# One decoder layer on one core: where the input and PLE tiles are turned, who makes the low parts of the second norm, and the loop order of the last gate

## The reference, cut to what matters

```python
x = x + (g_a * (y_a @ w_br_moba) + g_b * (y_b @ w_br_nsa)) @ w_o     # two branches, merge gates, output projection
u = causal_dwconv(rms_norm(x, ffn_norm) @ w_up, conv_w, conv_b)      # second norm, up projection, conv of 3
u_act, u_lin = split(u, 2)
x = x + (gelu(u_act) * u_lin) @ w_down
x = x + sigmoid(x @ w_ple_gate) * (p @ w_ple)                        # p is (512, 256)
```

## Time and profile before

| | us |
|---|---|
| median of 3 runs (lowest, highest) | 994.91 (992.62, 996.42) |
| the profiled execution | 993.43 |
| its span | 991.6 |
| TensorE busy in the span | 913.8 (92%) |
| VectorE, ScalarE, GpSimd busy | 485.4, 405.8, 381.8 |

### The profile page before, as it was taken

One profiled execution on the slowest core, in us unless ns is written; L12 is line 12 of the kernel. 1 busy time (PEld: TensorE's weight loads), 2 busy tenths in 40 slices (PEclk: granted clock), 3 DMA queues, 4 the chain that ended last, 5 costly groups with the idle time before them and its releaser, 6 DMA issues.

```text
span 991.6 us, 13260 instructions
## 1 busy us (share of the span) xinstructions
PE 913.8 (92%) x4581; PEld 779.1 (79%) x4581; DVE 485.4 (49%) x1145; ACT 405.8 (41%) x849; POOL 381.8 (38%) x360
## 2 busy tenths in 40 slices
PE   7898798786989889998989899999999999999988
PEld 7896688686978777877767678888888888888866
DVE  6616766767686677786431433444333342011132
ACT  5121554444454445554334354544444453232320
POOL 4723312303031211124545475444544445464540
PEclk9999899999989989999999999999999999999999
DMA  5745222214111212334554334333333333332232
GB/s 165 178 110 138 64 62 70 72 36 114 44 33 54 75 54 75 100 128 164 182 169 130 117 112 135 94 95 96 88 108 103 98 94 103 99 96 85 85 97 84
DMA packets 98917, 99.33 MB, mean 100 GB/s; under 512 B 15940, under 2 KB 73252, under 8 KB 98852
## 3 DMA queue, kind: packets, MB, share of 16 engines
q1 hardware_dynamic: 98799, 98.48, 33.9%
q10 hardware_dynamic: 53, 0.01, 0.0%
HBM read 87.58 MB, written 10.88 MB: 99 GB/s over the span
## 4 chain that ended last, share of the span: by engine, by line
PE 78%; DVE 12%; issue 4%; ACT 4%; DMA 1%; POOL 0%; SPq 0%; POOLq 0%; ACTq 0%; DVEq 0%
PE banks L1411 24%; PE banks L1413 23%; PE banks L1412 23%; DVE plain_arena L1161 2%; PE banks L1542 2%; PE banks L1460 1%; DVE plain_arena L1189 1%; DVE split_arena L1080 1%; DVE split_arena L1234 1%; PE banks L1525 1%; PE banks L1524 1%; ACT split_arena L836 1%; PE banks L1484 1%; DMA plain_arena<-in_x_dram 1%; ACT plain_arena L824 1%
## 5 line engine op out<-in xcount | busy, mean ns | idle before, releaser
L1411 PE MATMUL banks<-split_arena 128*128 128x512 f32 (+4 forms) x1224 | 471.3, 385 | 15.7 <-POOL split_arena L652 4.1
L1413 PE MATMUL banks<-split_arena 128*128 128x512 f32 (+4 forms) x1224 | 459.1, 375 | 0.0
L1412 PE MATMUL banks<-split_arena 128*128 128x512 f32 (+4 forms) x1224 | 458.6, 375 | 0.0
L652 POOL TENSOR_TENSOR split_arena<-plain_arena,split_arena 128x512 fp32r<-128x512 f32 x184 | 238.7, 1309 | 248.5 <-ACT split_arena L852 248.5
L1411 PEld LDWEIGHTS banks<-split_arena 128*128 128x128 f32 x1224 | 234.6, 192 | 58.8 <-issue 12.4
L1413 PEld LDWEIGHTS banks<-split_arena 128*128 128x128 f32 x1224 | 233.4, 191 | 36.3
L1412 PEld LDWEIGHTS banks<-split_arena 128*128 128x128 f32 x1224 | 234.5, 192 | 32.7
L852 ACT ACTIVATE split_arena<-plain_arena 128x512 fp32r<-128x512 f32 x184 | 113.3, 628 | 196.3 <-PE banks L1413 187.8
L824 ACT ACTIVATE plain_arena<-plain_arena 128x128 f32<-128x128 f32 (+1 forms) x96 | 53.9, 561 | 135.7 <-DVE plain_arena L1189 135.5
L1372 DVE SCALAR_TENSOR_TENSOR plain_arena<-banks,plain_arena 128x511 f32<-128x511 f32 x44 | 32.7, 744 | 135.3 <-ACT plain_arena L954 135.3
L620 POOL TENSOR_TENSOR split_arena<-plain_arena,split_arena 128x512 fp32r<-128x512 f32 x16 | 26.5, 1655 | 155.8 <-ACT split_arena L910 143.5
(11 more groups left out here) (158 smaller groups left out, 868.1 us busy)
## 6 DMA issues: line engine op xcount, KB each, us to landing
plain_arena<-in_w_up_dram SPq DMA_DIRECT2D x88, 256.0 KB, 3.2
plain_arena<-in_w_down_dram SPq DMA_DIRECT2D x44, 256.0 KB, 2.6
plain_arena<-in_w_in_dram SPq DMA_DIRECT2D x18, 512.0 KB, 4.4
plain_arena<-in_w_in_dram SPq DMA_DIRECT2D x32, 192.0 KB, 3.3
plain_arena<-in_x_dram SPq DMA_DIRECT2D x8, 512.0 KB, 4.7
gates<-plain_arena SPq DMA_DIRECT2D x16, 256.0 KB, 2.0
plain_arena<-skew SPq DMA_DIRECT2D x16, 256.0 KB, 3.7
plain_arena<-gates SPq DMA_DIRECT2D x16, 256.0 KB, 3.7
```

Source lines behind the costliest of these rows:

```text
L652: pool.tensor_tensor(W2l[:, c % RING, :], raw2[:, c % RING, :], W2h[:, c % RING, :].bitcast(F32), ALU.subtract).then_inc(w2_lo, 1)
L1411: nc.tensor.matmul(o, ah, bh, start=first, stop=False)
L1412: nc.tensor.matmul(o, ah, bl, start=False, stop=False)
L1413: return nc.tensor.matmul(o, al, bh, start=False, stop=last)
```

## The change

**x and p.** Tiles 0 and 1 of x are loaded into the columns of `x1T` that belong to tokens 256 to 511, as soon as attention no longer needs that memory (`turned` T). They are turned ahead of chunks 10 and 11, the first into banks 4 and 5, the second into banks 6 and 7, both behind `brB_done` 4. Tile 2 uses `xs` and is turned ahead of step 2 of `wo` half 0 behind `brB_done` 8, p is turned ahead of step 3 into banks 6 and 7, tile 3 (buffer `xg`) ahead of step 5. The first chunk of branch B, half 1, now waits for four copies to `x1T` instead of two, and p is loaded at chunk 19 behind the second turned tile. **The second norm.** GpSimd waits, ahead of its split of chunk 39, until four low parts of the norm are made (`h2_lo` 4). These low parts, and those ahead of the last gate, are now made by VectorE. The sum of squares has one wide add less on VectorE, and `token_sums` takes the last tile of squares with four further matmuls. **The last gate.** ScalarE splits the chunk ahead of the tanh. Half 1 goes depth step by depth step over the four token tiles, the last of them as two halves of 256 columns (banks 7 and 0), and its last two steps tile by tile. The end has nine pieces instead of eight.

The diff, without unchanged lines, and without the renamed semaphores, banks and indices in `take_x`, `pTl` and the stores (which go over the same nine pieces):

```diff
@@ -154,6 +154,7 @@
     RING = 8
+    TAIL = [(k, slice(0, S)) for k in range(7)] + [(7, slice(0, 256)), (7, slice(256, 512))]
@@ -391,6 +392,21 @@
     return ("k", n % 2, x - 2) if n < 4 else ("k", (n - 4) // 2, x - 2)
...
+def x_again(tt):
...
+    if tt < 2:
+        return x1T[:, :, (2 + tt) * P:(3 + tt) * P]
+    return (xs if tt == 2 else xg).rearrange("p (k c) -> p k c", k=KT)
...
+p_nat = x1T[:, :, 3 * P:4 * P]
...
+def tail_bank(k, cs):
...
+    return k if cs.start == 0 else 0
...
+def x_bank(tt):
+    return (4, 6, 4, 4)[tt]
@@ -535,22 +551,19 @@
-        if tt in (1, 3):
-            sp.wait_ge(xs_tr, tt if tt == 1 else 2)
-        if tt == 2:
-            sp.wait_ge(br_sum, 8)
-            sp.dma_start(xg, x_d[tt]).then_inc(xg_in, 16)
-        else:
-            sp.dma_start(xs, x_d[tt]).then_inc(xs_in, 16)
+        sp.dma_start(x_again(tt), x_d[tt].rearrange("p (k c) -> p k c", k=KT)).then_inc(xr_in[tt], 16)
...
+    sp.wait_ge(turned, T)
+    load_x(0)
+    load_x(1)
...
-    load_x(0)
+    load_x(2)
@@ -564,17 +577,15 @@
         if c == 19:
-            load_x(1)
+            sp.wait_ge(xs_tr, 2)
+            for tt in range(NT):
+                sp.dma_start(p_nat[:, 2 * tt:2 * tt + 2, :], p_d[tt].rearrange("p (k c) -> p k c", k=2)).then_inc(p_in, 16)
...
-            load_x(2)
+            sp.wait_ge(br_sum, 8)
...
-        if c == 28:
-            sp.wait_ge(xs_tr, 3)
-            for tt in range(NT):
-                sp.dma_start(xg[:, tt * PLE:(tt + 1) * PLE], p_d[tt]).then_inc(xg_in, 16)
@@ -711,6 +723,8 @@
                                    ALU.subtract).then_inc(yt_lo[0], 1)
+            if c == cidx[("wo", 1, KT - 1)] + RING:
+                pool.wait_ge(h2_lo, 4)
@@ -723,16 +737,6 @@
                         pool.tensor_tensor(sumsq, sumsq, sqt[:, kt % 2, :], ALU.add).then_inc(ssq_done, 1)
-        if c == cidx[("ple", 1, 0)] + 7:
-            for kt in range(KT):
-                pool.wait_ge(h2_hi, kt + 1)
-                pool.tensor_tensor(h2l[:, kt, :], hst[:, kt % 2, :], h2h[:, kt, :].bitcast(F32), ALU.subtract).then_inc(h2_lo, 1)
-        for mg in range(2):
-            if c == cidx[("dn", mg, NF - 1)] + 7:
-                for m in range(4):
-                    kt = 4 * mg + m
-                    pool.wait_ge(x2_hi, kt + 1)
-                    pool.tensor_tensor(h2l[:, kt, :], x1T[:, kt, :], h2h[:, kt, :].bitcast(F32), ALU.subtract).then_inc(x2_lo, 1)
@@ -973,21 +977,21 @@
     for c in range(RING, NC + 10):
-        if c == 11 + RING:
-            take_x(0)
...
+        if e in (10, 11):
+            take_x(e - 10)
...
-        if kind == "wo" and a == 0 and kt in (2, 4, 5):
-            take_x({2: 1, 4: 2, 5: 3}[kt])
-        if kind == "wo" and a == 0 and kt == 7:
+        if kind == "wo" and a == 0 and kt in (2, 5):
+            take_x({2: 2, 5: 3}[kt])
+        if kind == "wo" and a == 0 and kt == 3:
...
-                nc.scalar.activation(pTh[:, k, :], PS[:, 4 + k, :], ACT.Copy).then_inc(pT_hi, 1)
+                nc.scalar.activation(pTh[:, k, :], PS[:, 6 + k, :], ACT.Copy).then_inc(pT_hi, 1)
@@ -1023,21 +1027,20 @@
                 nc.scalar.activation(h2h[:, i, :], x1T[:, i, :], ACT.Copy).then_inc(x2_hi, 1)
+        if c < NC:
+            split_chunk(c)
...
-            for tt in range(NT):
-                k = 4 * a + tt
+            for k, cs in TAIL[:4] if a == 0 else TAIL[4:]:
...
-                    act.wait_ge(tail_done, tt + 1)
+                    act.wait_ge(tail_done, TAIL.index((k, cs)) - 3)
...
-                nc.scalar.activation(thb[:, k % 4, :], PS[:, 4 * a + tt, :], ACT.Tanh, scale=0.5).then_inc(th_done, 1)
-        if c < NC:
-            split_chunk(c)
+                nc.scalar.activation(thb[:, k % 4, cs], PS[:, tail_bank(k, cs), cs], ACT.Tanh, scale=0.5).then_inc(th_done, 1)
@@ -1343,12 +1346,12 @@
-    for a, b, n in ((0, 1, 6), (2, 3, 8)):
-        dve.wait_ge(x1_sq, n)
-        link(nc.vector.tensor_tensor(sqt[:, a, :], sqt[:, a, :], sqt[:, b, :], ALU.add))
-    link(nc.vector.tensor_tensor(sqt[:, 0, :], sqt[:, 0, :], sqt[:, 2, :], ALU.add))
+    dve.wait_ge(x1_sq, 6)
+    link(nc.vector.tensor_tensor(sqt[:, 0, :], sqt[:, 0, :], sqt[:, 1, :], ALU.add))
...
-    nc.vector.tensor_tensor(sumsq, sumsq, sqt[:, 0, :], ALU.add).then_inc(sq_summed, 1)
+    link(nc.vector.tensor_tensor(sumsq, sumsq, sqt[:, 0, :], ALU.add))
+    dve.wait_ge(x1_sq, 7)
+    nc.vector.tensor_tensor(sumsq, sumsq, sqt[:, 2, :], ALU.add).then_inc(sq_summed, 1)
@@ -1356,11 +1359,16 @@
     dve.wait_ge(bc_done, 1)
-    for i in range(KT):
-        if i >= 2:
-            dve.wait_ge(h2_lo, i - 1)
-        nc.vector.scalar_tensor_tensor(out=hst[:, i % 2, :], in0=x1T[:, i, :], scalar=cst[:, 8 + i:9 + i], in1=rbc,
-                                       op0=ALU.mult, op1=ALU.mult).then_inc(h2_f, 1)
+    for i in range(KT + 1):
+        if i < KT:
+            if i >= 2:
+                dve.wait_ge(h2_lo, i - 1)
+            nc.vector.scalar_tensor_tensor(out=hst[:, i % 2, :], in0=x1T[:, i, :], scalar=cst[:, 8 + i:9 + i], in1=rbc,
+                                           op0=ALU.mult, op1=ALU.mult).then_inc(h2_f, 1)
+        if i > 0:
+            kt = i - 1
+            dve.wait_ge(h2_hi, kt + 1)
+            nc.vector.tensor_tensor(h2l[:, kt, :], hst[:, kt % 2, :], h2h[:, kt, :].bitcast(F32), ALU.subtract).then_inc(h2_lo, 1)
@@ -1388,20 +1396,23 @@
             nc.vector.tensor_tensor(x1T[:, i, :], PS[:, 4 * mg + m, :], x1T[:, i, :], ALU.add).then_inc(x2_done, 1)
+        for kt in range(4 * mg, 4 * mg + 4):
+            dve.wait_ge(x2_hi, kt + 1)
+            nc.vector.tensor_tensor(h2l[:, kt, :], x1T[:, kt, :], h2h[:, kt, :].bitcast(F32), ALU.subtract).then_inc(x2_lo, 1)
...
-    for k in range(8):
+    for i, (k, cs) in enumerate(TAIL):
...
-        dve.wait_ge(th_done, k + 1)
+        dve.wait_ge(th_done, i + 1)
...
-        nc.vector.scalar_tensor_tensor(out=thb[:, k % 4, :], in0=thb[:, k % 4, :], scalar=1.0, in1=ppb[:, k % 4, :],
+        nc.vector.scalar_tensor_tensor(out=thb[:, k % 4, cs], in0=thb[:, k % 4, cs], scalar=1.0, in1=ppb[:, k % 4, cs],
...
-        dve.wait_ge(th_mul, k + 1)
+        dve.wait_ge(th_mul, i + 1)
...
-        o = x2n[:, tt, ng * 512:(ng + 1) * 512]
-        nc.vector.tensor_tensor(o, o, thb[:, k % 4, :], ALU.add).then_inc(o_done, 1)
+        o = x2n[:, tt, ng * 512 + cs.start:ng * 512 + cs.stop]
+        nc.vector.tensor_tensor(o, o, thb[:, k % 4, cs], ALU.add).then_inc(o_done, 1)
@@ -1631,36 +1642,30 @@
     def turn_x(tt):
-        if tt == 2:
-            pe.wait_ge(xg_in, 16)
-        else:
-            pe.wait_ge(xs_in, 16 * (tt + 1 if tt < 2 else 3))
-        src = xg if tt == 2 else xs
-        b = 4 + 2 * (tt % 2)
-        if tt == 0:
-            pe.wait_ge(brB_done, 4)
-        if tt >= 1:
-            pe.wait_ge(brB_done, 8)
-        if tt >= 2:
-            pe.wait_ge(xT_done, 2 * tt - 2)
+        pe.wait_ge(xr_in[tt], 16)
+        b = x_bank(tt)
+        pe.wait_ge(brB_done, 4 if tt < 2 else 8)
+        if tt == 3:
+            pe.wait_ge(xT_done, 6)
...
-            ins = nc.tensor.transpose(PS[:, b + kt // 4, P * (kt % 4):P * (kt % 4 + 1)], src[:, P * kt:P * (kt + 1)], ident)
+            ins = nc.tensor.transpose(PS[:, b + kt // 4, P * (kt % 4):P * (kt % 4 + 1)], x_again(tt)[:, kt, :], ident)
...
-        pe.wait_ge(xg_in, 16 * 5)
-        pe.wait_ge(xT_done, 8)
+        pe.wait_ge(p_in, 16 * NT)
+        pe.wait_ge(brB_done, 8)
...
-                ins = nc.tensor.transpose(PS[:, 4 + k, P * tt:P * (tt + 1)], xg[:, tt * PLE + P * k:tt * PLE + P * (k + 1)], ident)
+                ins = nc.tensor.transpose(PS[:, 6 + k, P * tt:P * (tt + 1)], p_nat[:, 2 * tt + k, :], ident)
...
-        pe.wait_ge(x1_done, KT)
+        pe.wait_ge(x1_sq, KT)
...
-            ins = nc.tensor.matmul(PS[:, 4, tt:tt + 1], sumsq[:, P * tt:P * (tt + 1)], ones[:, 0:1], start=True, stop=True)
+            nc.tensor.matmul(PS[:, 4, tt:tt + 1], sumsq[:, P * tt:P * (tt + 1)], ones[:, 0:1], start=True, stop=False)
+            ins = nc.tensor.matmul(PS[:, 4, tt:tt + 1], sqt[:, 3, P * tt:P * (tt + 1)], ones[:, 0:1], start=False, stop=True)
@@ -1685,16 +1690,14 @@
                 turn_probs(T + c - LAG)
-        if c == 10:
-            turn_x(0)
-        if (kind, a, kt) == ("wo", 0, 1):
-            turn_x(1)
+        if c in (10, 11):
+            turn_x(c - 10)
+        if (kind, a, kt) == ("wo", 0, 2):
+            turn_x(2)
...
-            turn_x(2)
+            turn_p()
...
-        if (kind, a, kt) == ("wo", 1, 0):
-            turn_p()
@@ -1723,7 +1726,7 @@
                 if a:
-                    pe.wait_ge(xT_done, 2)
+                    pe.wait_ge(xT_done, 4)
@@ -1734,6 +1737,7 @@
                     pe.wait_ge(pT_lo, 2)
+                    pe.wait_ge(xT_done, 8)
@@ -1783,13 +1787,21 @@
+    def last_gate(kt, k, cs):
...
+        w_, t_ = cidx[("pg", 1, kt)] % RING, slice(P * (k - 4), P * (k - 3))
+        if kt == 0 and tail_bank(k, cs) == 0:
```

(33 more changed lines are left out.)

2 lines of the change are left out of this document (1 added, 1 removed).

## The result

| | us |
|---|---|
| changed kernel, median of 4 runs (lowest, highest) | 979.61 (977.41, 981.22) |
| kernel before, same session, median of 4 | 993.76 (992.43, 996.42) |
| ratio | 0.9849, 95% interval 0.983 to 0.9867 |
| profiled execution, its span | 978.59, 976.8 |

The change is worth 14.8 us by the two profiled executions (14.2 by the medians). 980.4 was forecast.

What follows compares the result with a forecast made beforehand. TensorE's work (78% of the span) plus its halts was taken as the bound. Terms 3.4 + 2.0 + 2.8 + 5.5 = 13.7 us gave 979.7 from the profiled execution and 981.2 from the median; forecast 980.4, range 976 to 987.

Steps and rivals of the forecast that it cites:

- parts 1 and 2: Turning x tiles and p around branch B and `wo`: x gains 4.4 us and gives back 1.0, p gains 2.0.
- part 3: Second norm: GpSimd held, one add fewer, low parts on VectorE; `up` starts 2.8 us sooner, bounds 1.5 and 3.2.
- part 4: Last gate: early split and new loop order remove the 4.09 us halt; 5.5 us gained, between 4.9 and 5.9.
- Part 1, the second halt: TensorE's halt before `turn_x(1)` shrinks from 3.98 to 1.26 us, clock stays up: 2.7 plus 1.7, together 4.4 us.
- Part 1, the price in the DMAs: One more MB of x delays GpSimd's splits before the gate loads, blocking a VectorE add: 1.0 us lost, bounds 0 and 2.0.
- part 2: p turned five chunks earlier, removing the wait before `wo` half 1: 2.0 us gained, bounds 1.8 and 2.2.
- Both covers: In the first `up` chunks, splits of chunks 39 and 42 are ready 3 us before TensorE needs them.
- rival C: The hold stops TensorE in the first `up` chunks, 3 us of halt with a low clock behind: 985.5; chance 0.06.
- A: Clock falls at one of two halts remaining around the x turns, 1.7 us plus up to 1.5 more halt: 983.6; chance 0.14.
- B: In the last gate, matmuls of 256 columns cost as much as 512: 985.5; chance 0.05.
- D: Slower than before: x tiles crowd the queues, TensorE halts ahead of chunk 8; 1000 needs 4 + 19 us late; chance 0.02.
- E: At the second x turn `brB_done` 8 moves later by as much as TensorE gains, 4.4 us less: 984.8; chance 0.07.

Runs made afterwards that it cites:

- u3: Changed kernel with tile 2 of x turned ahead of step 1 of `wo` half 0 instead of step 2; ratio to the kernel before 0.9888.
- u2: Changed kernel without the hold of GpSimd ahead of its split of chunk 39; ratio to the kernel before 0.9839.
- u6: Changed kernel with the second norm's low parts on GpSimd at their old place and no hold; ratio to the kernel before 0.9859.
- i5: Changed kernel with x tile 1 loaded behind the load of chunk 15 and tile 2 behind that of chunk 20; ratio to the kernel before 0.9842.
- u4: Changed kernel with the second norm's low parts on GpSimd, among its splits of chunks 39 to 42, a hold kept; ratio to the kernel before 0.9877.
- u1: Changed kernel with the last gate's half 1 again token tile by token tile, early split and halved tile kept; ratio to the kernel before 0.9861.
- i2: Changed kernel with x tiles 0 and 1 turned ahead of chunk 11, tile 2 ahead of `wo` step 3, p ahead of step 4; ratio 0.9821.

## Why the prediction was right, point by point

The forecast was 13.7 us: 5.4 for parts 1 and 2, 2.8 for part 3, 5.5 for part 4. The profiles show 6.0 (stretch a), 3.1 (b) and 5.25 (d), 0.24 in the last store, and 0.2 ahead of stretch a: 14.8 in all. The 0.2 are not the change's, since the clock fell in attention in the profile of before and not in that of after (last section). The mechanisms held. Single sizes were off in both directions and partly made up for each other.

- *Part 1, the second halt.* Forecast 1.26 us and no fall of the clock; measured 1.04 and 1.00. u3 shows both prices. The ground given for the clock, halts of 1.97 us and less without a fall, was weaker than it looked: in u2 and u6 it fell behind a halt of 0.25 us and one-column matmuls.
- *Part 1, the price in the DMAs.* The mechanism is shown by i5. It was sized at 1.0 us, as one add blocked for a whole split. In this profile it was two adds with 0.36 and 0.39 us, 0.6 us in all at the first turned tile; over the eight profiles it was 0.3 to 1.1 us. The delay of GpSimd's splits was sized wrong the other way: 1.2 us said, 3.0 measured (470.18 to 473.20), just over the bound of 2.9. Counted from the first matmul behind attention's halt at 451 us it is 2.0 to 3.1 us in the eight. So two thirds or more of the 2.9 us for the extra MB was paid, and the free 19% of the queues took little of it. The gate loads came late for the same reason, but the first four gated products (a wait of 1.40 us at 469.88) were still done 5.7 us ahead of their use.
- *Parts 1 and 2 together.* 5.4 us said, 6.0 measured (stretch a). The price was 0.4 too high and the second halt 0.2 too long. Within part 2 the 0.24 us for refilling sets the length of one matmul (0.47) against the distance between two (0.2265). From start to start it was 0.30 (535.23 to 535.53), so 0.08, which leaves the 2.0 as it is. That p's halt went is seen in the trace alone; its undoing wasn't tried, because p now lies in memory that tile 3 is copied into.
- *Part 3.* 2.8 said, 3.07 measured (stretch b). The sixteen records of `token_sums` took 1.8 us, not 1.95. u2 gives the hold 1.6 us, and u6 against u2 gives the last hop 0.6, as priced. The Trainium skill's page Perfetto Trace Analysis (Optimizing Scalar/DVE Operations) says of moving work between the two engines only that it might not help. Read as a price of 0, as in the prediction, it does not fit: the first low part takes 0.69 us on VectorE in u2 and 1.26 on GpSimd in u6, with GpSimd held in neither. Both covers held in the changed kernel: chunk 42, for one, was split at 578.90 and needed at 565.52 + 6 x 2.72 = 581.8. But u4 shows how near rival C was: the danger was not GpSimd's own time but the loads and stores that SyncE had queued behind it, a path the prediction did not follow.
- *Part 4.* 5.5 said, 5.25 in stretch d, and the last store was 0.24 us shorter. TensorE took 22.2 us for half 1 (22.1 said), but the first tanh started 0.34 us after the point at which the sum had its tile full (968.27 against 950.03 + 17.9), so the last add ended 2.4 us behind the last matmul, not 2.1. What the prediction did not separate is that the split's place brings most of the gain, together with the halved tile (u1), and that the clock (half of 3.2 us, 1.6) fell behind the halt of 4.09 us and not behind the 2.21 of u1.
- *Rivals.* A, no: the clock stayed at 1.00 behind 1.61 us here, and behind 1.32 to 2.12 in the other profiles of the same code. B, no: matmuls of 256 columns stood 0.12 us apart. C, no in this kernel; in u4 2.6 us of it came, at full clock. D, no: TensorE did not halt ahead of chunk 8. E, no: the second halt did shrink, by 2.9 us.
- *Slips in the working that change nothing.* The five halts are seven values. Part 4's own terms add up to 983.6, not 983.7. The 23 us of rival D are eight times the bound of 2.9, not six.

## What to carry to other kernels

Where engines run in program order, a halt is the distance between an event and the place of the work that needs it: count the chunks of independent work between them and move the place, as i2 did for 2.8 us with no operation changed. Before holding an engine back, follow what other queues wait for behind it (here splits, then SyncE's loads, then stores, then copies), for the hold paid only together with moving that engine's other job. And place work on GpSimd by what VectorE does in that microsecond, since even a tiny operation of VectorE (128 x 4) took 1.26 us instead of 0.16 during a split.
